# Even layer of a two-part block: the sparse attention's indexer moved ahead of its other projections, and the memory units of the recurrence moved

## The reference

```python
h = xn @ even_w_in                       # 256 x 4240: A_COLS of the sparse attention, then the recurrence
c_q, c_kv, k_rope, k_idx, w_idx = split_cols(h, [512, 256, 32, 64, 16])
c_q, c_kv, k_idx = rms_norm of each;  k_rope, k_idx rotated
q     = c_q @ w_uq                       # 8 heads x 128, 32 of each rotated
q_idx = rope(c_q @ w_qidx)               # 16 indexer heads x 64
score = sum_h w_idx[h] * relu(q_idx[h] @ k_idx.T)      # 256 x 256, masked by chunks of 64
sel   = top_k(score, 64)                 # the keys that the attention may see
p     = softmax((q_nope @ (w_uk c_kv) + q_rope @ k_rope) * scale) over sel
y_a   = p @ c_kv @ w_uv
y_b   = rwkv7_mixer(h[..., A_COLS:])     # decay, keys and gates by low-rank products, then a scan over time
x     = x + concat(y_a, y_b) @ even_w_out
kv    = rms_norm(mem) @ xattn_wkv[layer] # keys and values of the memory, for the attention that follows
```

## Time and profile before

| | us |
|---|---|
| median of 3 runs | 4339.6 (4339.18 to 4341.56) |
| the profiled execution, its own time | 4340.11 |
| its span | 4338.3 |
| TensorE busy | 4014.0 (93%) |
| VectorE busy | 2208.7 (51%) |
| ScalarE busy | 1663.8 (38%) |
| stretch of the even layer that the change touches | about 1761 to 2004 from the span's start |
| mean granted TensorE clock | 0.946 |

### The profile page before, as it was taken

The page is one execution under the profiler, slowest core; times in us unless marked ns, Lnnn a source line. Parts: engine busy times, 40 slices in busy tenths (PEclk is TensorE's granted clock), DMA queues, the critical chain, the costliest instruction groups (busy, mean ns, idle before and its releaser), DMA issues. The chain is left out here.

```text
span 4338.3 us, 50003 instructions
## 1 busy us (share of the span) xinstructions
PE 4014.0 (93%) x20145; PEld 3127.7 (72%) x20145; DVE 2208.7 (51%) x3264; ACT 1663.8 (38%) x2300; POOL 154.1 (4%) x273
## 2 busy tenths in 40 slices
PE   5699999999899899887889999999986899999998
PEld 2466667778787688544777888888875777888887
DVE  6711125453555667375365554455456555544554
ACT  4221123232344354331234553454452455533543
POOL 2000001000000000002200000000000000000000
PEclk9799999999999999997679999999987999999999
DMA  9566555312365277433244666665651545656664
GB/s 356 189 210 212 190 189 181 98 64 97 112 199 150 75 221 223 127 115 100 76 134 131 180 186 193 183 185 188 226 192 46 183 151 162 187 190 188 184 199 160
DMA packets 353220, 719.17 MB, mean 166 GB/s; under 512 B 25036, under 2 KB 27416, under 8 KB 348520
## 3 DMA queue, kind: packets, MB, share of 16 engines
q1 hardware_dynamic: 331872, 637.74, 46.7%
q0 software_dynamic: 19472, 76.35, 5.2%
q10 hardware_dynamic: 1672, 2.24, 0.1%
HBM read 686.33 MB, written 26.48 MB: 164 GB/s over the span
## 5 line engine op out<-in xcount | busy, mean ns | idle before, releaser
L2286 DVE TENSOR_TENSOR ring_r<-ring,ring_r 128x1024 fp32r<-128x1024 f32 (+1 forms) x984 | 1188.4, 1218 | 1604.0 <-ACT ring_r L1546 1593.8
L1546 ACT ACTIVATE ring_r<-ring 128x1024 fp32r<-128x1024 f32 (+1 forms) x984 | 1029.3, 1053 | 1797.4 <-DMA ring<-in_w_in 581.7
L881 PE MATMUL acc<-ring_r,feat_hi 128*128 128x512 f32 x5120 | 1602.0, 394 | 36.1 <-DVE ring_r L2286 11.6
L881 PEld LDWEIGHTS acc<-ring_r,feat_hi 128*128 128x128 f32 x5120 | 957.6, 189 | 287.5 <-DVE ring_r L2286 37.5
L881 PE MATMUL acc<-ring_r,feat_lo 128*128 128x512 f32 x2560 | 1001.3, 391 | 0.0
L881 PE MATMUL acc<-ring_r,hid_t_hi 128*128 128x512 f32 x2048 | 631.5, 389 | 0.0
L881 PEld LDWEIGHTS acc<-ring_r,feat_lo 128*128 128x128 f32 x2560 | 483.4, 189 | 103.1
L881 PEld LDWEIGHTS acc<-ring_r,hid_t_hi 128*128 128x128 f32 x2048 | 383.7, 188 | 79.4
L881 PE MATMUL acc<-ring_r,hid_t_lo 128*128 128x512 f32 x1024 | 398.5, 389 | 0.0
L881 PE MATMUL acc<-ring_r,feat_e_hi 128*128 128x512 f32 (+1 forms) x1088 | 332.4, 388 | 17.0 <-DVEq L2376 9.5
L881 PEld LDWEIGHTS acc<-ring_r,feat_e_hi 128*128 128x128 f32 x1088 | 204.7, 191 | 58.4 <-issue 12.0
(11 more groups left out here) (475 smaller groups left out, 3276.4 us busy)
## 6 DMA issues: line engine op xcount, KB each, us to landing
ring<-in_ffn_up SPq DMA_DIRECT2D x256, 512.0 KB, 3.7
ring<-in_ffn_down SPq DMA_DIRECT2D x256, 512.0 KB, 3.6
ring<-in_w_mod SPq DMA_DIRECT2D x192, 512.0 KB, 5.6
ring<-in_w_in SPq DMA_DIRECT2D x176, 512.0 KB, 3.8
ring<-in_w_out SPq DMA_DIRECT2D x64, 512.0 KB, 3.6
ring<-in_even_w_in SPq DMA_DIRECT2D x64, 512.0 KB, 4.5
ring<-in_xattn_wkv SPq DMA_DIRECT2D x32, 512.0 KB, 4.4
ring<-in_even_w_out SPq DMA_DIRECT2D x32, 512.0 KB, 4.2
```

The source lines that it names most:

```text
L881: mm = pe.matmul(bank[0:l.shape[-1], 0:width], l, r, start=(kk == 0 and j == 0), stop=(kk == g.kt - 1 and j == len(terms) - 1))
L1546: f(ring_r[:, slot, 0, 0:kt, 0:width], ring[:, slot, 1, 0:kt, 0:width], ACT.Copy) \
L2286: tt(lo, raw, hi, ALU.subtract).then_inc(sem("w_lo"), E.up("w_lo"))
```

## The change

- The list of products has the indexer's queries first, then the values, then the attention's queries.
- TensorE's order is now: `g_qi`, `g_uv`, the transposes of the indexer's queries of both tiles, the 16 logits, the keys, `g_uq`, the memory's transposes, the transposes of the attention's queries, `attend`.
- VectorE posts the first `dsa_part` ahead of `mix(8)`; it rotates the indexer's queries of both tiles, adds up the scores of both tiles, then selects for both, and only then rotates the attention's queries.
- ScalarE follows: relus behind the values, then keys, the memory's sums, the attention's queries, the memory's copies, sigmoid and tanh, attention.
- The recurrence's tile t has `mem_kv(0, t, 0)` in its first wait and `mem_kv(0, t, 1)` in its second; the memory's transposes for layer 1 stand behind both tiles, on TensorE, ScalarE and VectorE.
- POOL waits only for `bias_ready`, posted behind the transposed attention's queries, before it loads the low-rank weights.

The diff, cut to its core (a line of three dots marks what is left out):

```diff
...
-        g.append(Gemm("uq", flat(W("dsa_w_uq_2", 0)), 512, chunks(0, 1024), 2, "act_free", split=False))
         g.append(Gemm("qidx", flat(W("dsa_w_qidx_2", 0)), 512, chunks(0, 1024), 2, "act_free", split=False))
         g.append(Gemm("uv", flat(W("dsa_w_uv_2", 0)), 256, chunks(0, 1024), 2, "act_free", split=False))
+        g.append(Gemm("uq", flat(W("dsa_w_uq_2", 0)), 512, chunks(0, 1024), 2, "act_free", split=False))
...
                     dma(mem_raw(t, h), I["mem_2"][0, t * P:(t + 1) * P, h * 1024:(h + 1) * 1024], "mem_in")
-            pool.wait_ge(sem("kt_ready"), L.due("kt_ready"))
+            pool.wait_ge(sem("bias_ready"), L.due("bias_ready"))
...
             dma(w_w2[64:128, :], I["rwkv_a2_2"][0], "w2_in")
-            pool.wait_ge(sem("bias_ready"), L.due("bias_ready"))
             for j, name in ((0, "w0"), (3, "a0")):
                 dma(w_row[:, j], row(I[f"rwkv_{name}_2"][0], B_W), "w2_in")
...
...
                 pe.wait_ge(sem("dsa_part"), E.due("dsa_part"))
-                gemm(g_uq, feat_lhs(d_cqt))
                 gemm(g_qi, feat_lhs(d_cqt))
                 gemm(g_uv, feat_lhs(d_ckt))
+                pe.wait_ge(sem("dsa_part"), E.due("dsa_part"))
+                for t in range(TT):
+                    for h in (0, 4):
+                        turn([d_qi[:, t, (h + j) * P:(h + j + 1) * P] for j in range(4)])
+                pe.wait_ge(sem("dsa_part"), E.due("dsa_part"))
+                for t in range(TT):
+                    for hp in range(8):
+                        bank = begin("act_free")
+                        pe.matmul(bank[:, :], d_qit[:, hp, t * P:(t + 1) * P], d_kit, start=True, stop=True) \
+                            .then_inc(sem("unit_full"), E.up("unit_full"))
...
+                gemm(g_uq, feat_lhs(d_cqt))
+                turn_mem()
+                pe.wait_ge(sem("dsa_part"), E.due("dsa_part"))
                 for t in range(TT):
-                    pe.wait_ge(sem("dsa_part"), E.due("dsa_part"))
                     for h in (0, 4):
                         turn([d_q[:, t, (h + j) * P:(h + j + 1) * P] for j in range(4)])
-                    for h in (0, 4):
-                        turn([d_qi[:, t, (h + j) * P:(h + j + 1) * P] for j in range(4)])
-                    if t == 0:
-                        turn_mem()
-                pe.wait_ge(sem("dsa_part"), E.due("dsa_part"))
-                for t in range(TT):
-                    for hp in range(8):
-                        bank = begin("act_free")
-                        pe.matmul(bank[:, :], d_qit[:, hp, t * P:(t + 1) * P], d_kit, start=True, stop=True) \
-                            .then_inc(sem("unit_full"), E.up("unit_full"))
-                pe.wait_ge(sem("mem_feat"), E.due("mem_feat"))
-                mem_kv(0, 0, 0)
                 pe.wait_ge(sem("bias_ready"), E.due("bias_ready"))
...
...
-                    mem_kv(0, t, 1)
+                    if t == 0:
+                        pe.wait_ge(sem("mem_feat"), E.due("mem_feat"))
+                    mem_kv(0, t, 0)
                     pe.wait_ge(sem("sig_ready"), E.due("sig_ready"))
...
                     mm.then_inc(sem("unit_full"), E.up("unit_full"))
-                    if t == 0:
-                        mem_kv(0, 1, 0)
-                    else:
-                        turn_mem()
+                    mem_kv(0, t, 1)
                     pe.wait_ge(sem("arbk_ready"), E.due("arbk_ready"))
...
+                turn_mem()
...
...
                 evac(g_in, to_hb)
-                act.wait_ge(sem("mix_done"), E.due("mix_done", len(MIX)))
-                evac(g_uq, lambda c, cs, t, bank: f(d_q[:, t, c * CH:(c + 1) * CH], bank, ACT.Copy) \
-                    .then_inc(sem("act_free"), E.up("act_free")))
-                mem_sums()
                 evac(g_qi, lambda c, cs, t, bank: f(d_qi[:, t, c * CH:(c + 1) * CH], bank, ACT.Copy) \
-                    .then_inc(sem("act_free"), E.up("act_free")))
-                evac(g_uv, lambda c, cs, t, bank: f(d_v[:, t, c * CH:(c + 1) * CH], bank, ACT.Copy) \
                     .then_inc(sem("act_free"), E.up("act_free")))
                 act.wait_ge(E.last_sem(), E.last_count())
                 act.nop().then_inc(sem("dsa_proj"), E.count("dsa_proj"))
-                for h in range(8):
-                    f(d_kt[:, h, :], take("unit_full")[:, 0:SEQ], ACT.Copy).then_inc(sem("act_free"), E.up("act_free"))
...
-                mem_turned(0)
+                evac(g_uv, lambda c, cs, t, bank: f(d_v[:, t, c * CH:(c + 1) * CH], bank, ACT.Copy) \
+                    .then_inc(sem("act_free"), E.up("act_free")))
                 slots = [stage[:, 0], stage[:, 1], prob[:, 0], prob[:, 1]]
...
                     act.wait_ge(E.last_sem(), E.last_count())
                     act.nop().then_inc(sem("rl_ready"), E.count("rl_ready"))
+                for h in range(8):
...
+                act.nop().then_inc(sem("kt_ready"), E.count("kt_ready"))
+                mem_sums()
+                act.wait_ge(sem("mix_done"), E.due("mix_done", len(MIX)))
+                evac(g_uq, lambda c, cs, t, bank: f(d_q[:, t, c * CH:(c + 1) * CH], bank, ACT.Copy) \
+                    .then_inc(sem("act_free"), E.up("act_free")))
+                act.wait_ge(E.last_sem(), E.last_count())
+                act.nop().then_inc(sem("dsa_proj"), E.count("dsa_proj"))
+                mem_turned(0)
                 act.wait_ge(sem("rl_used"), E.due("rl_used", 4))
-                act.wait_ge(sem("rstd_ready"), E.due("rstd_ready"))
...
-                mem_kv(0, 0, 0)
                 attend(dsa_units())
+                act.wait_ge(sem("rstd_ready"), E.due("rstd_ready"))
...
...
-                    mem_kv(0, t, 1)
+                    mem_kv(0, t, 0)
                     banks = [take("unit_full") for _ in range(3)]
-                    if t:
-                        mem_turned(1)
                     act.wait_ge(sem("einv_go"), E.due("einv_go"))
...
-                    if t == 0:
-                        mem_kv(0, 1, 0)
+                    mem_kv(0, t, 1)
+                mem_turned(1)
                 act.wait_ge(sem("kbv_out"), E.due("kbv_out", 16 * 6 * TT))
...
...
                 stream(g_in, each=under_product)
+                dve.wait_ge(E.last_sem(), E.last_count())
+                dve.nop().then_inc(sem("dsa_part"), E.count("dsa_part"))
                 mix(8)
                 dve.wait_ge(sem("even_h"), E.due("even_h", 7))
-                dve.wait_ge(E.last_sem(), E.last_count())
-                dve.nop().then_inc(sem("dsa_part"), E.count("dsa_part"))
-                for g in (g_uq, g_qi, g_uv):
-                    stream(g)
-                skip("unit_full", 8)
+                stream(g_qi)
                 dve.wait_ge(sem("dsa_proj"), E.due("dsa_proj"))
                 for t in range(TT):
-                    q = blocks(d_q[:, t], HD)
-                    rotate(q[:, :, 0:16], q[:, :, 16:32], trig[:, t, 0:16], trig[:, t, 24:40], d_tmp, 8, 16)
                     q = blocks(d_qi[:, t], 64)
                     rotate(q[:, :, 0:8], q[:, :, 8:16], trig[:, t, 16:24], trig[:, t, 40:48], d_tmp, 16, 8)
-                    dve.wait_ge(E.last_sem(), E.last_count())
-                    dve.nop().then_inc(sem("dsa_part"), E.count("dsa_part"))
-                    for dst in (d_qt, d_qit):
+                dve.wait_ge(E.last_sem(), E.last_count())
+                dve.nop().then_inc(sem("dsa_part"), E.count("dsa_part"))
+                stream(g_uv)
+
+                def turned_to(dst):
...
+
+                turned_to(d_qit)
                 dve.nop().then_inc(sem("dsa_part"), E.count("dsa_part"))
-                dve.wait_ge(sem("sd_ready"), E.due("sd_ready"))
-                dve.reciprocal(mem_rstd, stat2[:, 76:78]).then_inc(sem("rstd_ready"), E.up("rstd_ready"))
                 slots = [stage[:, 0], stage[:, 1], prob[:, 0], prob[:, 1]]
...
                             dve.wait_ge(E.last_sem(), E.last_count())
+                skip("unit_full", 16 + 8)
+                for t in range(TT):
                     for half in range(2):
...
                     ts(d_bias[:, t], d_bias[:, t], -1.0, 1e30, ALU.add, ALU.mult).then_inc(sem("dve_step"), E.up())
-                skip("unit_full", 16)
-                skip("gemm_full", 1)
-                dve.wait_ge(E.last_sem(), E.last_count())
+                stream(g_uq)
+                dve.wait_ge(sem("dsa_proj"), E.due("dsa_proj"))
+                for t in range(TT):
+                    q = blocks(d_q[:, t], HD)
+                    rotate(q[:, :, 0:16], q[:, :, 16:32], trig[:, t, 0:16], trig[:, t, 24:40], d_tmp, 8, 16)
+                dve.wait_ge(E.last_sem(), E.last_count())
+                dve.nop().then_inc(sem("dsa_part"), E.count("dsa_part"))
+                dve.wait_ge(sem("sd_ready"), E.due("sd_ready"))
+                dve.reciprocal(mem_rstd, stat2[:, 76:78]).then_inc(sem("rstd_ready"), E.up("rstd_ready"))
+                turn_skip(8)
```

(7 more changed lines are left out.)

27 lines of the change are left out of this document (13 added, 14 removed).

## The result

| | us |
|---|---|
| changed kernel, median of 5 runs | 4303.66 (4301.4 to 4309.56) |
| kernel before, median of 5 runs beside them | 4339.6 (4327.39 to 4345.7) |
| ratio | 0.9922, 95% interval 0.9904 to 0.994 |
| the profiled execution, its own time | 4302.13 |
| its span | 4300.0 |

Faster by 0.8%: 34 us by the ratio, 36 us by the medians. The prediction was 4307, and the sum of its terms 32.8 us.

The account below looks back on a forecast made before the run. Before the attention, the indexer's score and selection on VectorE were taken as the bound, delayed by all work ahead of the first logit. Terms summed to -32.8 us, 4306.8 from the median, stated as 4307, range 4296 to 4320.

Parts of the forecast that it names:

- the attention itself: Sparse attention from its first score on: not changed, so no gain or loss of its own.
- Term 1: TensorE's wait before the first projection ends after chunk 7's mix, falling from 9.0 to about 2 us: -6.9 us.
- Term 2: First projection to first logit: 48 instead of 80 records ahead, keeping 2.5 us of clock loss: -28.1 us.
- Term 3: First logit to the attention's first score: TensorE and ScalarE end last instead of VectorE, 42.7 against 37.1 us: +5.6 us.
- VectorE 3.9 us ahead: Before the attention's first score, VectorE was expected to finish 3.9 us ahead of TensorE and ScalarE.
- the 4 us of idle time that I named as a sign: VectorE was expected to stand idle some 4 us before the attention's first score, near 1833.
- Term 4: Recurrence's tile 0: ring loads lie on the stores of k, b and v: +1.5 us, between 0 and 4.
- Term 5: Recurrence's tile 1: last transposes end 5.9 us earlier, less 1 us for ring loads on the stores: -4.9 us.
- Term 6: Gate's products after tile 1: they keep the low clock, so 0, with -8.7 us as the bound.
- The rival: The gate's products run at 2.4 GHz: 8.7 us less, 4298 us in all; chance 0.18.
- the two signs that would have shown me wrong: First score later than 1840, or time from the last transposes to the gate's products growing above 10 us.

Follow-up runs that it names:

- experiment 3: Changed kernel with VectorE's signal for the first projection posted behind the mix of chunk 8 again; 4315.4 us, ratio 0.9952 to the kernel before.
- Experiments 1 and 4: Changed kernel with the recurrence's memory units and memory transposes put back, 4317.1 us; changed kernel with the values' products moved behind the indexer's logits, 4311.3 us.
- Experiment 5: Changed kernel with six idle matmuls where TensorE waits 4.65 us for the gate's weights; 4293.4 us, ratio 0.9892 to the kernel before.
- experiment 8: Changed kernel with triangular-system products ahead of the gate's, plus idle matmuls in the scan (three before the first chunk, one per chunk); 4288.0 us, ratio 0.9892.

## Why the prediction was right

Term by term, predicted and measured, in us:

| | predicted | measured |
|---|---|---|
| 1. first wait | -6.9 | -7.25 |
| 2. first projection to first logit | -28.1 | -29.63 |
| 3. first logit to first score | +5.6 | +5.76 |
| the attention itself | 0 | +0.37 |
| 4. stores against loads | +1.5 | +2.08 (two rows of the table: +0.02, +2.06) |
| 5. tile 1 | -4.9 | -4.26 |
| 6. clock of the gate's products | 0 | 0 |
| sum | -32.8 | -32.93 |

That the sum agrees to 0.1 us is luck: the terms are off by up to 1.5 us one way and 0.6 us the other, and the spread from execution to execution is larger than that.

- **Term 1** held, and experiment 3 confirms that it lies on the path about one to one (7.2 us more of waiting, 8.3 us more of stretch).
- **Term 2**: I kept a clock loss of 2.5 us. The 48 records took 22.46 us against 21.0 at full clock, so 1.5 were lost in this execution (0 in two others with the same wait), behind a wait of 1.7 us and not 9. With the wait back (experiment 3) 2.8 are lost. The rest of the 1.5 us by which the term was too small is the transposes and copies ahead of the first logit, 3.2 us instead of 3.6.
- **Term 3** held to 0.2 us, with its reason: VectorE's 35.9 us stayed, and TensorE's and ScalarE's work took over as the last to end. My "VectorE 3.9 us ahead" was wrong: it compares the end of its rotation with the first score, but TensorE's transposes and VectorE's copies of them come between. Against the start of these transposes its slack is 0.6 us at most, and the 4 us of idle time that I named as a sign did not come; it waits 0.91 us. Experiments 1 and 4 show the new bound.
- **Term 4** was right in sign and reason, and somewhat small. The stores alone keep the DMA engines 0.93 to 0.98 busy, and with the loads on top VectorE waits 2.06 us longer for them. The rule that I weighed, that transfers started by any engine run on the same 16 DMA engines and interleave (the Trainium skill, DMA: Bandwidth & Descriptors, "Issuing engines are not separate DMA queues"), agrees with the trace: 3.67 and 4.10 us of wait with the slots freed early, 5.2 to 6.2 us with them freed late.
- **Term 5**: the transposes start 4.0 us earlier, and the path from there to POOL's load is 1.9 us shorter (both as worked out). The load took 7.06 us from issue to TensorE's resumption instead of 5.38: I had allowed 1 us for the ring's loads beside it; it was 1.7 (the load takes 6.9 to 7.1 us in all four kernels of the table that have the new order in tile 1, 5.4 and 5.5 in the two that have the old one).
- **Term 6** came out at its value for a wrong reason, so its value is luck too. "They never brought the clock back" was true, but I took it for a property of the products. Experiment 5 shows the wait to be the cause. The rule of the Trainium skill (TensorE: Matmul & The Clock Gate, "What's actually happening"), that sustained activity releases the throttle, still disagrees with 17 us of nearly gapless work at 0.50; the same work keeps 1.00 where it starts with it. The rival lost not because the clock can't be had, but because the change leaves 4.65 us of waiting in front. I had written about 2 us for that wait; my own terms gave 3 (transposes done 5.9 us earlier, 4.4 us for the memory's, the load's end 4.9 us earlier), and the shorter transposes and the later load add the rest.

Of the two signs that would have shown me wrong, neither came: the first score is at 1833.8, below 1840, and from the end of the last transposes to the gate's first transpose the time grew from 6.6 to 9.1 us, below 10.

## What to carry to other kernels

When a vector chain is the bound, look for what stands ahead of its first operand, not beside it: the first logit came 30 us sooner after the first projection by order alone, since 32 projection records, the keys and the transposes could stand behind it, and 6 us of that went back because this work then ended last. Then ask what the engine that waited will be short of, because work that cost next to nothing in the cover (1.1 of 14 us here) costs nearly its full length (12.7 us) once the cover moves. And a wait costs more than its length where the matmuls behind it lose the clock: 4.65 us of waiting cost 8 more in the gate's products. Idle matmuls in that wait got 7.4 us back within the trace, and useful products in it, with the solve started earlier, 21.1 us.

## What was not expected of the hardware

- The granted clock depends on how a stretch is entered. The same gate's products took 17.3 us at 0.50 behind a wait of 4.65 us, and 9.5 us at 1.00 behind filler. They took 8.4 us at 1.00 behind the system's products, although these left waits of 0.3 to 0.5 us between them.
- In the scan of experiment 8 the granted clock fell from 1.00 to 0.50 while TensorE was busy without a gap, and stayed there from 2102 to 2118.
- A DMA share near 1 doesn't say how much is moved: the stores alone moved 244 GB/s at 0.98, and with the ring's loads on top 334 GB/s were moved at 1.01. A share over a window that begins ahead of the transfers reads too low: 0.59 from 1923 to 1931 in the kernel before, where they begin at about 1926.
